# Attention values in a decoder step: both halves of one head's values side by side in one stationary operand

## The chip, the cores and the metric

The kernel runs on one core of one Trainium2 chip. The metric is the device time of one execution in microseconds (us). TensorE is called PE below, VectorE DVE, ScalarE ACT, GpSimd POOL and SyncE SP, as in the profile.

## What is computed

One inference step of a two-layer decoder trunk: 1024 prompt tokens and 64 sample tokens (8 sequences of 8), model width 1024. Layer 0 mixes with sparse attention (8 query heads, 2 key/value heads of width 64, the 256 best keys of each query) beside a pooling mixer, layer 1 with a gated spatial unit, and each layer has a SwiGLU part with 2816 hidden columns. The change touches one product of layer 0, the probabilities times the values of the prompt:

```python
logits = jnp.where(valid, einsum('bnhgd,bnshd->bnhgs', qg, k_sel) * HEAD_DIM ** -0.5, -inf)
p = jax.nn.softmax(logits, axis=-1)
o = jnp.einsum('bnhgs,bnshd->bnhgd', p, v_sel)
```

## The kernel before

The work is cut into two groups of tokens, g = 0 (prompt tokens 0 to 511) and g = 1 (tokens 512 to 1023 and the 64 sample tokens). For each group the kernel runs the attention, then the output projection, then the SwiGLU part of layer 0, layer 1 and its SwiGLU part. Every engine has its own program, and semaphores order them. There is no scheduler: the order of each engine is the order of the code.

All large products are made in three parts. An fp32 number is split into a high part (a copy rounded to the type fp32r, which PE multiplies in one pass) and a low part (the number minus its high part), and PE adds high by high, high by low and low by high into one PSUM bank.

The prompt's attention (`attend`, one per engine) goes through tiles `t` of 128 queries, 0 to 3 in group 0 and 4 to 7 in group 1. A pair of a tile and a key/value head, (t, z) with z = 0 or 1, is called a *section* here: it holds four query heads, and t + 1 blocks `kk` of 128 keys. The table `items(g)` sets the order of the work on all engines:

- `qk`: the logits of one query head, on PE (L899 the mask, L902 the products), then on DVE the row maximum (L1916) and its negative (L1918), on ACT the exponential with its row sum (L1279), on DVE the reciprocal of the sum (L1898, held back for up to three items), on POOL the division of the row (L1618, the tiles `probs_short`, `probs_long_a` and `probs_long_b`). The four heads of the *next* section are put among the first blocks of the present one. They are called heads A, B, C, D below.
- `tr`: one block of the four heads' probabilities is transposed on PE (L912) into one of two PSUM banks, copied by ACT to the high part (L1303, tile `probs_t`), and DVE subtracts to make the low part (L1925, the same tile). The section's first transpose waits until POOL has divided head D.
- `pv`: PE multiplies the block by the values (L919, tile `values_split`) into bank 6 + z. It waits for the low part of its own block; the transpose of the block after it is issued ahead of it.
- `o`: the finished section's result, 64 rows of the bank, is written to `act_split`, the operand of the output projection: the high part by a copy of ACT (L1311), the low part by a subtraction of DVE (L1930). It stands in the *next* section, just behind that section's first `pv`; the last section's stands at the end.

In `pv` the stationary operand is a 128 by 128 block of the values, keys by (both key/value heads, 64 columns each). So PE makes 128 rows for each section, of which `o` takes the 64 of head z. The values are split once per group by ACT (L1264) and POOL (L1592). After the last `o`, group 0 goes on with the output projection (L653), group 1 with the sample tokens' attention (L935 and on), and both wait for it. A matmul of PE is called a product.

## Time and profile before

| | |
|---|---|
| time, median of 3 runs | 2970.72 us (2960.51 to 2972.42) |
| profiled execution: time | 2972.42 us |
| profiled execution: span | 2972.3 us |
| PE busy, products | 2648.4 us (89%) |
| PE busy, weight loads (beside the products) | 2328.3 us |
| DVE, ACT, POOL busy | 1453.8, 995.1, 1250.6 us |
| the 216 products of `pv` (L919), busy | 68.2 us |
| group 0's attention | about 420 to 498 us |
| group 1's attention (prompt part) | about 1592 to 1707 us |

The first column of the profile's group rows is the line of the kernel. "Busy" of a group is the time in which at least one of its instructions ran; a mean is of one instruction. The shares over the whole span say little on this change, since it touches 193 of 2972 us.

### The profile page before, as it was taken

How to read it: one execution, taken by the hardware profiler on the slowest of the kernel's cores; microseconds unless marked ns; L12 is line 12 of the kernel's file. 1: busy time of each engine (PE TensorE's matmuls, PEld its weight loads, DVE VectorE, ACT ScalarE, POOL GpSimd, SP SyncE). 2: the span in 40 equal slices, each digit the busy share in tenths (PEclk: the TensorE clock that was granted, in tenths of full speed). 3: DMA queues.
4: the chain of work that ended last, by engine and by line, in shares of the span. 5: the costliest groups of instructions: out<-in, count | busy, mean ns of one | idle time of the engine just before them, and what ended most of it. 6: DMA issues, size and time to landing. Idle time of an engine off the chain costs nothing.

```text
span 2972.3 us, 43500 instructions
## 1 busy us (share of the span) xinstructions
PE 2648.4 (89%) x15061; PEld 2328.3 (78%) x15065; DVE 1453.8 (49%) x1895; ACT 995.1 (33%) x1450; POOL 1250.6 (42%) x632
## 2 busy tenths in 40 slices
PE   6979767799997887999986897999997987999997
PEld 5669545588886665888865677999997987999997
DVE  3459755898688655312355635221235445220234
ACT  3242444432233344322224534222223334222222
POOL 4434223354553334554544413443443333443441
PEclk9979879799998888999988987999998988999998
DMA  4443211133232211333322121232232211232231
GB/s 120 100 122 83 81 45 32 56 93 105 86 103 81 64 50 57 93 103 94 100 63 85 35 81 50 80 92 76 78 89 60 71 51 45 78 88 78 81 94 51
DMA packets 451740, 230.00 MB, mean 77 GB/s; under 512 B 90588, under 2 KB 443568, under 8 KB 451127
## 3 DMA queue, kind: packets, MB, share of 16 engines
q1 hardware_dynamic: 451647, 228.80, 26.7%
q8 instruction: 53, 0.87, 0.1%
q14 instruction: 40, 0.33, 0.0%
HBM read 213.43 MB, written 15.43 MB: 77 GB/s over the span
## 4 chain that ended last, share of the span: by engine, by line
PE 72%; DVE 16%; issue 5%; ACT 3%; POOL 2%; DMA 1%; SPq 0%; DVEq 0%; ACTq 0%; POOLq 0%
PE psum L653 63%; DVE top L1715 2%; DVE scores L1722 2%; DVE temps L2027 1%; DVE square_sums L1678 1%; DVE resid L2032 1%; PE psum L741 1%; PE psum L685 1%; DVE scores L1860 1%; POOL act_split L1552 1%; DVE probs_t L1925 1%; PE psum L734 1%; PE psum L912 1%; DVE diag_rstd L1687 1%; DVE row_stats L1916 1%
## 5 line engine op out<-in xcount | busy, mean ns | idle before, releaser
L653 PE MATMUL psum<-act_split,w_hi 128*128 128x288 f32 (+1 forms) x6144 | 1368.5, 332 | 28.2 <-POOL act_split L1552 9.5
L1520 POOL TENSOR_TENSOR w_lo<-w_raw,w_hi 128x1024 fp32r<-128x1024 f32 (+1 forms) x336 | 859.5, 2558 | 1234.2 <-ACT w_hi L1096 1234.2
L653 PEld LDWEIGHTS psum<-act_split,w_hi 128*128 128x128 f32 x6144 | 998.0, 191 | 125.5 <-issue 19.1
L1096 ACT ACTIVATE w_hi<-w_raw 128x1024 fp32r<-128x1024 f32 (+1 forms) x336 | 376.9, 1122 | 1419.7 <-PE psum L653 1379.6
L653 PE MATMUL psum<-act_split,w_lo 128*128 128x288 f32 (+1 forms) x3072 | 844.1, 329 | 0.0
L653 PEld LDWEIGHTS psum<-act_split,w_lo 128*128 128x128 f32 x3072 | 527.5, 190 | 41.3
L653 PE MATMUL psum<-hidden_split,w_hi 128*128 128x288 f32 (+1 forms) x2112 | 461.3, 327 | 0.0
L653 PEld LDWEIGHTS psum<-hidden_split,w_hi 128*128 128x128 f32 x2112 | 339.6, 188 | 27.4
L653 PE MATMUL psum<-hidden_split,w_lo 128*128 128x288 f32 (+1 forms) x1056 | 287.7, 327 | 0.0
L1671 DVE TENSOR_TENSOR square_sums<-square_sums,squares 128x512 f32<-128x512 f32 (+1 forms) x80 | 167.9, 2099 | 168.5 <-ACT squares L1360 121.9
L1980 DVE TENSOR_TENSOR temps<-psum,root_of_input 128x512 f32<-128x512 f32 (+1 forms) x88 | 63.5, 721 | 360.0 <-PE psum L653 346.3
L1986 DVE TENSOR_TENSOR temps<-psum,temps 128x512 f32<-128x512 f32 (+1 forms) x88 | 63.4, 720 | 352.1 <-PE psum L653 333.4
L1988 DVE TENSOR_TENSOR hidden_split<-temps,hidden_split 128x512 f32 (+1 forms) x88 | 171.3, 1946 | 92.9 <-ACT hidden_split L1375 92.9
L653 PEld LDWEIGHTS psum<-hidden_split,w_lo 128*128 128x128 f32 x1056 | 179.5, 188 | 13.7
L1722 DVE MATCH_REPLACE8 scores<-top,scores 128x640 f32<-128x640 f32 (+2 forms) x208 | 178.0, 864 | 0.0
L685 PE MATMUL psum<-act_split,w_hi 128*128 128x288 f32 (+1 forms) x384 | 123.0, 417 | 57.5 <-POOL act_split L1552 31.9
L1715 DVE MAX8 top<-scores 128x8 f32<-128x640 f32 (+2 forms) x208 | 170.4, 869 | 2.1
L685 PEld LDWEIGHTS psum<-act_split,w_hi 128*128 128x128 f32 x384 | 78.6, 240 | 82.5 <-POOL act_split L1552 46.5
L1539 POOL TENSOR_TENSOR temps<-temps,root_of_input 128x512 f32<-128x512 f32 (+1 forms) x88 | 119.9, 1363 | 31.3 <-ACT temps L1372 31.2
L1552 POOL TENSOR_TENSOR act_split<-mixed,act_split 128x512 fp32r<-128x512 f32 (+1 forms) x48 | 71.5, 1491 | 110.8 <-ACT mixed L1402 110.8
L1925 DVE TENSOR_TENSOR probs_t<-psum,probs_t 128x512 fp32r<-128x512 f32 x72 | 49.3, 688 | 63.3 <-ACT probs_t L1303 63.0
L919 PE MATMUL psum<-probs_t,values_split 128*128 128x512 f32 x216 | 68.2, 427 | 10.9 <-DVE probs_t L1925 10.8
(240 smaller groups left out, 2392.4 us busy)
## 6 DMA issues: line engine op xcount, KB each, us to landing
w_raw<-in_w_ffn_gate_up SPq DMA_DIRECT2D x352, 256.0 KB, 3.1
w_raw<-in_w_ffn_down SPq DMA_DIRECT2D x64, 384.0 KB, 3.5
w_raw<-in_w_ffn_down SPq DMA_DIRECT2D x64, 320.0 KB, 4.0
w_raw<-in_w_in_even SPq DMA_DIRECT2D x64, 256.0 KB, 3.7
w_raw<-in_w_in_odd SPq DMA_DIRECT2D x64, 256.0 KB, 3.0
w_raw<-in_w_out_odd SPq DMA_DIRECT2D x32, 256.0 KB, 3.1
x_rows<-in_x_prompt SPq DMA_DIRECT2D x8, 512.0 KB, 6.3
w_raw<-in_w_out_even SPq DMA_DIRECT2D x32, 128.0 KB, 2.9
```

What stands on the lines that cost most here:

```text
L653: mm = pe.matmul(PS[:, 2 * p + b, 0:hi - lo], w[:, p, at], x(k)[:, lo:hi], start=(k == 0 and w is WH and x is x_hi), stop=(k == ph.kt - 1 ...
L685: mm = pe.matmul(PS[:, 2 * p + b, 0:hi - lo], w[:, p, at], x(k)[:, lo:hi], start=(k == 0 and w is WH and x is a_hi), stop=(k == ph.kt - 1 ...
L919: mm = pe.matmul(PS[:, 6 + z, :], VS[:, v, kk, :], PT[:, kc % 2, q, :], start=kk == 0 and v == 0 and q == 0, stop=kk == t and v == 1)
L1096: act.activation(WH[:, p, 0:n], WR[:, p, 0:n], ACT.Copy).then_inc(S("w_hi"), 1)
L1520: pool.tensor_tensor(WL[:, p, 0:n], WR[:, p, 0:n], WH[:, p, 0:n].bitcast(F32), ALU.subtract).then_inc(S("w_lo"), 1)
L1539: pool.tensor_tensor(TT[:, 0, 0:T[g]], TT[:, 0, 0:T[g]], RB[:, 0:T[g]], ALU.mult).then_inc(S("gated"), 1)
L1552: pool.tensor_tensor(AR[:, 1, n, 0:T[g]], src, AR[:, 0, n, 0:T[g]].bitcast(F32), ALU.subtract).then_inc(S("a_lo"), 1)
L1671: dve.tensor_tensor(SS[:, 0:T[g]], SS[:, 0:T[g]], SQ[:, p, 0:T[g]], ALU.add).then_inc(S("ss_p"), 1)
L1715: ins_ = dve.max(M8[0:s.shape[0], m, :], s)
L1722: ins_ = dve.match_replace(out=s, in_to_replace=M8[0:s.shape[0], m, :], in_values=s, imm_value=CHOSEN)
L1925: dve.tensor_tensor(PT[:, kc % 2, 1, :], PS[:, 4 + kc % 2, :], PT[:, kc % 2, 0, :].bitcast(F32), ALU.subtract).then_inc(S("pt_lo"), 1)
L1988: dve.tensor_tensor(flat(HR[:, 1, ds(i, 1), 0:T[g]]), TT[:, 1, 0:T[g]], flat(HR[:, 0, ds(i, 1), 0:T[g]].bitcast(F32)), ALU.subtract).then_ ...
```

## The change

The tile `VS` (`values_split`) gets another layout: keys by (block, key/value head, high or low, 64). The stationary operand of `pv` is now the high part and the low part of *one* head's values, side by side. Its 128 columns give, in rows 0 to 63 of the bank, the high values times the probabilities, and in rows 64 to 127 the low values times the probabilities. The moving operand goes through it twice, the high and then the low part of the probabilities: two products per block in place of three. The product of low by low comes with them, which was not computed before.

The two halves of the bank must then be added. In `o`, ACT copies rows 64 to 127 to a new tile `out_low`, DVE adds rows 0 to 63 to it and writes a new tile `out_total`, and from that ACT makes the high part and DVE the low part as before. The new tiles lie over `squares` and `temps`, which are free there.

```diff
-        VS = over("values_split", [P, 2, 8, P], F32R, h_at, 4096)
+        VS = over("values_split", [P, 8, 2, 2, HD], F32R, h_at, 4096)
+        OL = over("out_low", [HD, 2, 512], F32, sq_at, 0)
+        OT = over("out_total", [P, 512], F32, tt_at, 0)
...
@@ PE, pv
-                        for v, q in ((0, 0), (0, 1), (1, 0)):
-                            mm = pe.matmul(PS[:, 6 + z, :], VS[:, v, kk, :], PT[:, kc % 2, q, :],
-                                           start=kk == 0 and v == 0 and q == 0, stop=kk == t and v == 1)
+                        for q in (0, 1):
+                            mm = pe.matmul(PS[:, 6 + z, :], VS[:, kk, z, :, :], PT[:, kc % 2, q, :],
+                                           start=kk == 0 and q == 0, stop=kk == t and q == 1)
...
@@ ACT, o
+                        wait(act, S("o_lo"), 2 * t + z - 1)
+                        act.activation(OL[:, z, :], PS[HD:P, 6 + z, :], ACT.Copy).then_inc(S("o_part"), 1)
+                        act.wait_ge(S("o_sum"), 2 * t + z + 1)
                         act.activation(AR[64 * z:64 * z + 64, 0, 0:4, at],
-                                       PS[64 * z:64 * z + 64, 6 + z, :].rearrange("p (j q) -> p j q", j=4), ACT.Copy).then_inc(S("o_hi"), 1)
+                                       OT[64 * z:64 * z + 64, :].rearrange("p (j q) -> p j q", j=4), ACT.Copy).then_inc(S("o_hi"), 1)
...
@@ DVE, o
-                        dve.wait_ge(S("o_hi"), 2 * t + z + 1)
+                        dve.wait_ge(S("o_part"), 2 * t + z + 1)
+                        dve.tensor_tensor(OT[r, :], PS[0:HD, 6 + z, :], OL[:, z, :], ALU.add).then_inc(S("o_sum"), 1)
+                        dve.wait_ge(S("o_hi"), 2 * t + z + 1)
-                        dve.tensor_tensor(AR[r, 1, 0:4, at], PS[r, 6 + z, :].rearrange("p (j q) -> p j q", j=4),
+                        dve.tensor_tensor(AR[r, 1, 0:4, at], OT[r, :].rearrange("p (j q) -> p j q", j=4),
                                           AR[r, 0, 0:4, at].bitcast(F32), ALU.subtract).then_inc(S("o_lo"), 1)
```

The split of the values by ACT and POOL changes only in its output's layout.

How the instructions of ACT stand in section (5, 0), from its second block on, before (`act_split<-psum` is `o`, `probs_t` the copy of a block, `probs_long_b` the exponential of a head):

```order
581 L1303 ACTIVATE probs_t<-psum 128x512
582 L1279 ACTIVATE probs_long_b,row_stats<-psum,row_stats 128x768
583 L1311 ACTIVATE act_split<-psum 64x4x128
584 L1303 ACTIVATE probs_t<-psum 128x512
585 L1279 ACTIVATE probs_long_b,row_stats<-psum,row_stats 128x768
```

and now:

```order
590 L1306 ACTIVATE probs_t<-psum 128x512
591 L1282 ACTIVATE probs_long_b,row_stats<-psum,row_stats 128x768
592 L1315 ACTIVATE out_low<-psum 64x512
593 L1317 ACTIVATE act_split<-out_total 64x4x128
594 L1306 ACTIVATE probs_t<-psum 128x512
595 L1282 ACTIVATE probs_long_b,row_stats<-psum,row_stats 128x768
```

`o` is two instructions in place of one, with a wait for DVE between them, and the copy of the next block and the exponential of head B stand behind both.

The same place on DVE, before (`row_stats` by TENSOR_REDUCE is a row maximum, by RECIPROCAL the inverse of a row sum):

```order
712 L1916 TENSOR_REDUCE row_stats<-psum 128x1
713 L1918 TENSOR_SCALAR row_stats<-row_stats 128x1
714 L1898 RECIPROCAL row_stats<-row_stats 128x1
715 L1930 TENSOR_TENSOR act_split<-psum,act_split 64x4x128
716 L1925 TENSOR_TENSOR probs_t<-psum,probs_t 128x512
717 L1898 RECIPROCAL row_stats<-row_stats 128x1
718 L1916 TENSOR_REDUCE row_stats<-psum 128x1
```

and now:

```order
721 L1922 TENSOR_REDUCE row_stats<-psum 128x1
722 L1924 TENSOR_SCALAR row_stats<-row_stats 128x1
723 L1904 RECIPROCAL row_stats<-row_stats 128x1
724 L1936 TENSOR_TENSOR out_total<-psum,out_low 64x512
725 L1938 TENSOR_TENSOR act_split<-out_total,act_split 64x4x128
726 L1931 TENSOR_TENSOR probs_t<-psum,probs_t 128x512
727 L1904 RECIPROCAL row_stats<-row_stats 128x1
728 L1922 TENSOR_REDUCE row_stats<-psum 128x1
```

The addition has come in ahead of the subtraction, the subtraction now waits for ACT's second instruction, and head B's reciprocal and head C's maximum stand behind both.

## Rows read from the trace of the kernel before

**Rows 1.** Windows: both attentions, then three stretches of group 0's; busy us (count), clock.
```profile
core 0: us, PE busy (x) PEld busy (x) DVE busy (x) ACT busy (x) POOL busy (x), PEclk, DMA share, GB/s
420.00:498.00 78.00, 51.33 (x228) 37.99 (x230) 41.62 (x123) 37.63 (x94) 30.64 (x38) 0.80 0.09 25
1592.00:1707.00 115.00, 100.83 (x530) 77.86 (x532) 74.97 (x147) 66.19 (x122) 53.62 (x35) 0.98 0.10 28
430.00:440.00 10.00, 6.63 (x25) 5.20 (x25) 3.76 (x14) 3.98 (x12) 3.71 (x5) 0.50 0.11 29
440.00:450.00 10.00, 7.76 (x27) 5.98 (x27) 5.27 (x16) 4.66 (x13) 3.72 (x5) 0.50 0.00 0
450.00:460.00 10.00, 6.07 (x34) 4.71 (x34) 5.37 (x16) 5.61 (x14) 4.58 (x5) 0.96 0.46 132
```

**Rows 2.** Waits of PE within group 1's attention: us in total, times, longest.
```profile
PE psum L919 <- DVE probs_t L1925: 7.8, 19, 1.1
PE psum L912 <- POOL probs_long_a L1618: 7.3, 3, 5.2
PE psum L912 <- POOL probs_long_b L1618: 2.0, 3, 1.1
```

**Rows 3.** Timeline of PE: one block's three products; the last two of them alone.
```profile
1654.56 0.85 PE L919 MATMUL psum<-probs_t,values_split 128*128 128x512 f32 x3
1654.79 0.62 PE L919 MATMUL psum<-probs_t,values_split 128*128 128x512 f32 x2
```

**Rows 4.** Chain of waits through section (5, 0): start us, us, what; then its end.
```profile
1623.21 0.88 DVE row_stats L1916
...
1624.37 0.69 DVE act_split L1930
...
1625.09 0.69 DVE probs_t L1925
...
1625.86 0.87 DVE row_stats L1916
...
1631.00 1.48 POOL probs_long_b L1618
```

**Rows 5.** Timeline around `o` in section (5, 0): start us, us, engine, line, operation.
```profile
1623.03 0.59 ACT L1311 ACTIVATE act_split<-psum 64x512 fp32r<-64x512 f32 x1
1623.64 0.60 ACT L1303 ACTIVATE probs_t<-psum 128x512 fp32r<-128x512 f32 x1
...
1624.30 0.90 ACT L1279 ACTIVATE probs_long_b<-psum,row_stats 128x768 f32<-128x768 f32 x1
...
1624.48 1.47 POOL L1618 TENSOR_TENSOR probs_long_b<-probs_long_b,row_stats 128x768 f32<-128x768 f32 x1 [2.35 <-DVE row_stats L1898]
...
1625.70 0.15 DVE L1898 RECIPROCAL row_stats<-row_stats 128x1 f32<-128x1 f32 x1
```

**Rows 6.** Timeline around `o` in section (0, 1) of group 0.
```profile
435.81 0.57 ACT L1311 ACTIVATE act_split<-psum 64x512 fp32r<-64x512 f32 x1
...
436.28 0.46 ACT L1279 ACTIVATE probs_short<-psum,row_stats 128x256 f32<-128x256 f32 x1
436.41 0.68 DVE L1930 TENSOR_TENSOR act_split<-psum,act_split 64x512 fp32r<-64x512 f32 x1 [0.37 <-ACT act_split L1311]
```

**Rows 7.** One line each: durations in ns, minimum, median and maximum.
```profile
L1272 ACT ACTIVATE queries_split<-queries_tile x16: 615/627/631, 415.3 to 1662.3; 64x512 fp32r<-64x512 f32 x16
L1671 DVE TENSOR_TENSOR square_sums<-square_sums,squares x80: 692/2319/3247, 14.0 to 2943.6; 128x512 f32<-128x512 f32 x40, 128x576 f32<-128x576 f32 x40
```

**Rows 8.** Timeline: a POOL instruction and a DVE one with two SBUF inputs beside it.
```profile
506.50 2.40 POOL L1520 TENSOR_TENSOR w_lo<-w_raw,w_hi 128x1024 fp32r<-128x1024 f32 x1 [17.33 <-ACT w_hi L1096]
...
507.24 2.20 DVE L1671 TENSOR_TENSOR square_sums<-square_sums,squares 128x512 f32<-128x512 f32 x1 [8.83 <-ACT squares L1360]
```

**Rows 9.** Timeline after the last block of group 1: `o`, then the next stage.
```profile
1705.72 0.59 ACT L1311 ACTIVATE act_split<-psum 64x512 fp32r<-64x512 f32 x1 [1.78 <-PE psum L919]
1706.35 0.69 DVE L1930 TENSOR_TENSOR act_split<-psum,act_split 64x512 fp32r<-64x512 f32 x1 [1.68 <-ACT act_split L1311]
1707.14 1.06 PE L935 MATMUL psum<-constants,key_pages 128*128 128x128 f32 x8 [1.46 <-issue]
```

More of the change, by code:

```diff
@@ L1263, in split_keys @@
                         act.activation(KS[64 * r:64 * r + 64, kv, 0, 0:n], KT[64 * kv:64 * kv + 64, 0:n], ACT.Copy).then_inc(S("ks_hi"), 1)
-                act.activation(VS[:, 0, 0:4 * (g + 1), :], VN[:, 0:4 * (g + 1), :], ACT.Copy).then_inc(S("ks_hi"), 1)
+                act.activation(VS[:, 0:4 * (g + 1), :, 0, :], VN[:, 0:4 * (g + 1), :].rearrange("p k (z d) -> p k z d", z=2),
+                               ACT.Copy).then_inc(S("ks_hi"), 1)
             def attend(g):
@@ L1591, in split_keys @@
                 pool.wait_ge(S("ks_hi"), 5 * g + 5)
-                pool.tensor_tensor(VS[:, 1, 0:4 * (g + 1), :], VN[:, 0:4 * (g + 1), :], VS[:, 0, 0:4 * (g + 1), :].bitcast(F32),
-                                   ALU.subtract).then_inc(S("ks_lo"), 1)
+                pool.tensor_tensor(VS[:, 0:4 * (g + 1), :, 1, :], VN[:, 0:4 * (g + 1), :].rearrange("p k (z d) -> p k z d", z=2),
+                                   VS[:, 0:4 * (g + 1), :, 0, :].bitcast(F32), ALU.subtract).then_inc(S("ks_lo"), 1)
                 pool.wait_ge(S("ks_lo"), 5 * g + 5)
```

## The prediction

> **What bounds the kernel now.** I read the windows first. Group 0's attention takes 78 us and PE computes in 51.3 of them; group 1's takes 115 us and PE computes in 100.8 [rows 1]. So fewer products look like a gain in group 1, and DVE (75 of 115) and ACT (66) look free. Then the waits: in group 1 PE waits 7.8 us in `pv` for the low part from DVE, and 9.3 us at the start of sections (7.3 and 2.0) for POOL's division [rows 2]. PE is thus often kept, not keeping. The chain of waits says by whom. Through section (5, 0) it runs on DVE without a gap: maximum of head B at 1623.21, `o` at 1624.37, low part of the block at 1625.09, maximum of head C at 1625.86, in the end POOL's division of head D at 1631.00 to 1632.48, which the next section's first transpose waits for [rows 4]. No product of `pv` is on it. A section lasts as long as this: logits of four heads, maxima, exponentials, reciprocals, four divisions. DVE and ACT are idle at the start and the end of a section and have no slack in its middle, which is where `o` stands.
>
> **The change part by part.** The sum is made against the profiled execution's 2972.42 us, 1.7 us over the median of 2970.72.
>
> *Products removed.* The second and third product of a block take 0.62 us of 0.85, so the second starts 0.23 us after the first: one product is 0.23 us of PE [rows 3]. 72 blocks lose one each: 20 x 0.23 = 4.6 us in group 0, 52 x 0.23 = 12.0 us in group 1, 16.6 together (somewhat more where the clock is at 0.50). That is the most that can be gained. On the path it counts only where PE goes from block to block with no head's logits between: the last section of each group, which prepares no other. There the blocks go in pairs, one `pv` of each pair on the path: 4 blocks give 2 x 0.23 = 0.5 us, 8 blocks 4 x 0.23 = 0.9 us. For section (4, 0), which has no `o`, I add 0.2. Gain: 1.6 us.
>
> *`o` in the middle of a section.* This is 6 sections in group 0 ((0, 1) to (3, 0)) and 6 in group 1 ((4, 1) to (7, 0)). I place the new instructions on the rows of (5, 0) [rows 4, 5]. ACT's copy to `out_low` costs what `o` costs ACT now, 1623.03 to 1623.62. DVE's addition, with one input in PSUM as now, stands where L1930 stands, 1624.37, and takes 0.69, to 1625.06. Until then ACT, which used to copy the next block at 1623.64, stands still. Then come ACT's copy from SBUF, 0.63 by the same form in L1272 [rows 7], to 1625.72; the block's copy, 0.60, to 1626.34; head B's exponential, 0.90 in place of 1624.30, and its sum, to about 1627.3. DVE can take head B's reciprocal at 1627.35 where it did at 1625.70 [rows 5], and head C's maximum right behind. That is 1.65 us later, and everything after it is serial: maximum C, maximum D, exponential, division, next section. By the same working the others of group 1 come to between 1.6 and 2.1, I take 1.7: 6 x 1.7 = 10.2 us.
> In group 0, section (0, 1): the first copy is done at 436.38; DVE adds from 436.41 to 437.09; ACT's second copy ends at 437.75; head D's exponential starts there and not at 436.28, 1.5 us later [rows 6]. The DVE side alone gives 1.3 (0.69 and 0.63 with the semaphores). I take 1.4: 6 x 1.4 = 8.4 us.
> Bounds for one of these twelve: below, 0 (all of it in idle time, as the shares of DVE and ACT in rows 1 would allow); above, 2.1 plus a wait for POOL, next.
>
> *The subtraction's inputs.* L1930 had one input in PSUM; its successor has both in SBUF. The nearest rows are L1671, also with two SBUF inputs: 0.69 us at least, but 2.32 in the median and 3.25 at most [rows 7]. The one at 507.24 ended at 509.44, 0.54 us after the POOL instruction beside it [rows 8]. In group 1, POOL divides head A's row just then (1624.48 to 1625.95 in rows 5), so the subtraction would end at about 1626.5 and the block's low part at 1627.2, just inside the 1627.35 above. I take 0.4 us over all sections; the upper bound is a division of 1.47 us more in each of six, 9 us.
> The Trainium skill (SBUF — State Buffer, Who interferes with whom) says that a DVE instruction with two SBUF inputs and a GpSimd instruction that reads SBUF exclude each other for the whole of an instruction, whichever came first. It thus speaks against this change; without it the sum would be 0.4 us less, by its worst case 9 more.
>
> *`o` in the two last sections.* In (3, 1) and (7, 1) the first copy need not wait long, and the following block comes about 0.4 us later: 0.8 together. After the last block `o` is bare: now 0.59 and 0.69, then PE goes on at 1707.14 [rows 9]. With a copy of 0.59, the addition 0.69, a copy 0.63 and the subtraction 0.69, it is longer by 1.3 us and one hand-over more, say 1.35. Twice: 2.7 us.
>
> *The split of the values* has the same sizes and comes long before the first product that reads it; I cost it at nothing. If the new layout doubled it, the load of queries that PE waits for would still cover it. The new waits for `o_lo` in ACT and PE ask for an `o` two sections back.
>
> Sum: 10.2 + 8.4 + 0.4 + 0.8 + 2.7 - 1.6 = 20.9 us. Against the profiled execution that is 2993.3, against the median 2991.6, so **2992 us**.
>
> **The rivals.**
> *PE bounds (faster than forecast, not slower than before).* If PE's 100.8 of 115 us is what sets group 1, all the removed products come off, 16.6 us, and only the bare ends cost, 2.7: -13.9, 2957 us. For it: PE's share, and that in sections (5, 1), (6, 1) and (7, 0) the chain runs over PE for a stretch. Against it: DVE starts each maximum there the moment the one before is through. It decides if ACT's and DVE's 1.3 us fit before the next logits are ready. Chance 0.07.
> *Half absorbed.* The delay in each of the twelve is only the bare work, about 0.6 us, and the later blocks give back 3 us in all: 7.2 + 3.5 - 1.6 - 3 = 6, 2977 us. For it: the section's last blocks have slack on DVE. Against it: their slack lies behind the delayed maxima. Chance 0.15.
> *The clock.* Group 0 runs at 0.50 (1.2 GHz) from 430 to 450 and is at 0.96 (2.4 GHz is 1.00) from 450 on, right after the slice in which PE was busiest, 7.76 of 10 us [rows 1]. With fewer products and longer waits the rise may come only with the output projection. A product is 0.287 us at half clock (7.76 / 27) and 0.179 after (6.07 / 34); of the 228 products some 150 lie behind 450 us: 16 us of PE, about half on the path, so +8: 3000 us. In group 1 PE would still be busy in 89 of about 125 us, more than the 6.07 of 10 that held the clock, so I leave that out. Chance 0.13.
> The Trainium skill (TensorE: Matmul & The Clock Gate, HAM oscillation — how this bites in real kernels) tells of kernels whose clock falls again in each gap between bursts of products. By that rule group 0 would not have risen at 450 us amid its gaps, so the trace does not bear it out fully here.
> *The port.* The subtraction waits for POOL each time, or holds it up: +9, 3001 us. Chance 0.07.
> That the change does not do what it says I exclude: the order shows two products per block and the longer `o` in both programs.
>
> **How the numbers follow.** The forecast has 0.58, with 15 to 26 us around its 21 (each of the twelve between 1.2 and 2.1). A measurement of this kernel tells about 0.5% from no change, 14.9 us, so slower starts at 2985.6. Of the forecast I leave 0.07 under that. Slower: 0.51 + 0.13 + 0.07 = 0.71. Faster by over 0.5% is under 2955.9: 0.03 of the 0.07 of the first rival. Within: 0.26. The range, 2974 to 3004, takes in the clock, the port and most of the half absorbed case with the scatter of the runs (2960.5 to 2972.4), and leaves out the first rival.
>
> **What would show it.** Sections of group 0 1.2 to 1.5 us longer, those of group 1 1.6 to 2.1 us, both attentions together about 213 us in place of 193; L919's successor at 144 products; PE's wait for POOL at the starts of sections grown, to over 15 us in group 1; the chain through a section going over ACT's second copy or the addition; nothing changed outside. I am wrong if the section's length does not grow, if the subtraction takes over 1.5 us on average, or if the granted clock after 450 us stays at half.

## The result and the profile after

The changed kernel takes 3005.93 us in the median of 4 runs (2996.08 to 3009.39), beside 2971.57 us for the kernel before (4 runs, 2960.51 to 2976.09). The ratio is 1.0121, interval 1.0087 to 1.0156: slower, as forecast, by 34.4 us where 20.9 were forecast, and 1.9 us above the upper end of the range.

The two profiled executions are compared by their spans, 2972.3 and 3003.9 us, which is 31.6 us more. The busy times after the change:

```profile
PE 2653.1 (88%) x14990; PEld 2329.1 (78%) x14993; DVE 1467.3 (49%) x1911; ACT 1005.9 (33%) x1466; POOL 1250.5 (42%) x632
```

PE has 72 products fewer, and its busy time is not shorter (2653.1 us, before 2648.4). So a part of what is left must run more slowly. The line of `pv` by itself (durations in ns: minimum, median, maximum), and PE's waits in group 1's attention, which answer to [rows 2] (there 7.8, 7.3 and 2.0 us):

```profile
L921 PE MATMUL psum<-probs_t,values_split x144: 387/397/796, 428.5 to 1733.7; 128*128 128x512 f32 x144
```

```profile
PE psum L921 <- DVE probs_t L1931: 12.8, 19, 1.6
PE psum L914 <- POOL probs_long_a L1624: 9.0, 4, 5.5
PE psum L914 <- POOL probs_long_b L1624: 3.1, 3, 1.5
```

144 products in place of 216. PE's wait for the low part has grown from 7.8 to 12.8 us, and that for POOL from 9.3 to 12.1.

The next view is cut at the moments at which POOL ends a section's fourth division, the end of a section as the prediction described it. The first six rows are sections (0, 1) to (3, 0) of group 0, the others (4, 1) to (7, 0) of group 1:

```profile
core 0: us, PE busy (x) PEld busy (x) DVE busy (x) ACT busy (x) POOL busy (x), PEclk, DMA share, GB/s
430.82:440.99 10.17, 4.87 (x18) 3.61 (x18) 4.44 (x15) 4.66 (x12) 3.71 (x6) 0.50 0.10 27
440.99:451.79 10.80, 5.16 (x24) 4.09 (x24) 5.95 (x17) 5.08 (x13) 3.71 (x6) 0.82 0.00 0
451.79:463.03 11.24, 5.85 (x24) 4.54 (x24) 5.62 (x16) 5.74 (x13) 4.58 (x6) 0.80 0.41 119
463.03:475.08 12.05, 7.75 (x30) 6.00 (x30) 7.11 (x18) 6.10 (x14) 4.57 (x5) 0.77 0.00 0
475.08:487.55 12.47, 7.70 (x29) 5.39 (x30) 6.89 (x17) 6.64 (x14) 5.42 (x5) 0.79 0.00 1
487.55:500.44 12.89, 9.57 (x36) 6.48 (x36) 7.65 (x18) 6.50 (x14) 4.16 (x4) 0.76 0.01 1
1620.89:1634.66 13.77, 9.42 (x54) 7.40 (x54) 9.06 (x19) 8.55 (x16) 7.15 (x6) 1.00 0.07 20
1634.66:1649.98 15.32, 10.57 (x60) 8.19 (x60) 10.38 (x21) 9.01 (x17) 7.16 (x6) 0.99 0.01 2
1649.98:1666.74 16.76, 12.67 (x60) 9.58 (x60) 10.45 (x20) 9.39 (x17) 7.99 (x5) 0.91 0.06 16
1666.74:1685.59 18.85, 15.39 (x66) 11.49 (x66) 12.06 (x22) 9.97 (x18) 7.99 (x5) 0.82 0.15 43
1685.59:1702.14 16.55, 13.02 (x66) 9.30 (x66) 11.84 (x21) 10.41 (x18) 8.86 (x6) 1.00 0.09 24
1702.14:1720.75 18.61, 14.27 (x71) 10.16 (x72) 12.62 (x22) 10.49 (x18) 7.57 (x4) 1.00 0.02 6
```

Two things are to be seen. Each of these twelve sections is longer than before, and the clock (last column but two) is well below 1.00 in eight of them, all of group 0 and (5, 1) and (6, 0). The same cuts in the kernel before, and in experiment e3 below, in which the clock was higher over both attentions, but not in (1, 0) and hardly in (2, 0):

| section | before: us, clock | change: longer by, clock | e3: longer by, clock | forecast |
|---|---|---|---|---|
| (0, 1) | 8.64, 0.50 | 1.53, 0.50 | 1.37, 0.99 | 1.4 |
| (1, 0) | 9.81, 0.50 | 0.99, 0.82 | 1.06, 0.53 | 1.4 |
| (1, 1) | 9.83, 0.88 | 1.41, 0.80 | 0.52, 0.98 | 1.4 |
| (2, 0) | 10.35, 1.00 | 1.70, 0.77 | 1.71, 0.78 | 1.4 |
| (2, 1) | 10.20, 1.00 | 2.27, 0.79 | 2.20, 0.95 | 1.4 |
| (3, 0) | 10.36, 1.00 | 2.53, 0.76 | 1.28, 1.00 | 1.4 |
| (4, 1) | 12.20, 1.00 | 1.57, 1.00 | 1.58, 1.00 | 1.7 |
| (5, 0) | 13.62, 1.00 | 1.70, 0.99 | 1.68, 1.00 | 1.7 |
| (5, 1) | 14.03, 1.00 | 2.73, 0.91 | 1.55, 1.00 | 1.7 |
| (6, 0) | 14.44, 1.00 | 4.41, 0.82 | 1.81, 1.00 | 1.7 |
| (6, 1) | 15.03, 1.00 | 1.52, 1.00 | 2.42, 1.00 | 1.7 |
| (7, 0) | 16.98, 1.00 | 1.63, 1.00 | 2.23, 1.00 | 1.7 |

**The hand-over.** The timeline around `o` in section (5, 0), which answers to [rows 5]:

```profile
1638.83 0.59 ACT L1315 ACTIVATE out_low<-psum 64x512 f32<-64x512 f32 x1
...
1640.18 0.69 DVE L1936 TENSOR_TENSOR out_total<-psum,out_low 64x512 f32<-64x512 f32 x1
...
1640.30 1.47 POOL L1624 TENSOR_TENSOR probs_long_b<-probs_long_b,row_stats 128x768 f32<-128x768 f32 x1 [2.35 <-DVE row_stats L1904]
...
1640.90 0.63 ACT L1317 ACTIVATE act_split<-out_total 64x512 fp32r<-64x512 f32 x1 [1.48 <-DVE out_total L1936]
1641.55 0.60 ACT L1306 ACTIVATE probs_t<-psum 128x512 fp32r<-128x512 f32 x1
1641.56 0.75 DVE L1938 TENSOR_TENSOR act_split<-out_total,act_split 64x512 fp32r<-64x512 f32 x1 [0.69 <-ACT act_split L1317]
1642.17 0.90 ACT L1282 ACTIVATE probs_long_b<-psum,row_stats 128x768 f32<-128x768 f32 x1
...
1643.28 0.94 DVE L1922 TENSOR_REDUCE row_stats<-psum 128x1 f32<-128x768 f32 x1
```

ACT writes `out_low` from 1638.83 to 1639.42 and then stands for 1.48 us, until DVE, which first takes head B's maximum, has added. Head B's exponential, for which the negative maximum is there from 1640.07 on, starts at 1642.17, and head C's maximum at 1643.28. From ACT's first instruction of `o` to head C's maximum it is 4.45 us; before, it was 1623.03 to 1625.86 [rows 4, 5], 2.83. That is 1.62 us, with 1.65 forecast by the same steps. The chain of waits of the change goes over just these instructions:

```profile
1641.55 0.60 ACT probs_t L1306
...
1642.17 1.00 ACT probs_long_b L1282 x2
...
1643.36 0.87 DVE row_stats L1922
```

**The clock.** Where it falls in group 1 the timeline of PE shows, at the end of section (5, 0), and the windows around it:

```profile
1646.77 0.73 PE L921 MATMUL psum<-probs_t,values_split 128*128 128x512 f32 x2 [0.53 <-DVE probs_t L1931]
1648.35 0.73 PE L921 MATMUL psum<-probs_t,values_split 128*128 128x512 f32 x2 [0.84 <-DVE probs_t L1931]
1650.03 1.11 PE L914 MATMUL psum<-constants,probs_long_b 128*128 128x128 f32 x4 [0.95 <-POOL probs_long_b L1624]
...
1651.38 1.90 PE L904 MATMUL psum<-keys_split,queries_split 128*128 128x448 f32 x4
```

```profile
1640.00:1650.00 10.00, 5.44 (x29) 3.65 (x27) 6.49 (x15) 5.72 (x11) 5.87 (x4) 0.98 0.00 0
1650.00:1653.00 3.00, 2.97 (x10) 2.52 (x11) 0.69 (x1) 1.22 (x2) 0.43 (x1) 0.50 0.00 0
1653.00:1660.00 7.00, 5.63 (x33) 4.43 (x32) 5.91 (x11) 4.99 (x9) 2.84 (x3) 1.00 0.13 37
```

After three waits in a row of 0.53, 0.84 and 0.95 us, with two products between one and the next, PE runs at 0.50, 1.2 GHz, for some 3 us: the four products of 1651.38 take 1.90 us. Afterwards it is at 1.00, 2.4 GHz, again. In the kernel before no section of this group after (4, 0) is below 1.00. The row of waits alone does not decide it: in e2 below, PE's same three waits at the end of (5, 0) are 0.54, 0.84 and 0.96 us, and the clock stays at 1.00. And the fall within (6, 0), from 1676.9 to 1680.3 us, came after one wait of 2.20 us in the section's middle.

**After the last block.** The timeline that answers to [rows 9]:

```profile
1734.11 0.59 ACT L1315 ACTIVATE out_low<-psum 64x512 f32<-64x512 f32 x1 [1.54 <-PE psum L921]
1734.73 0.68 DVE L1936 TENSOR_TENSOR out_total<-psum,out_low 64x512 f32<-64x512 f32 x1 [1.45 <-ACT out_low L1315]
...
1735.45 0.63 ACT L1317 ACTIVATE act_split<-out_total 64x512 fp32r<-64x512 f32 x1 [0.75 <-DVE out_total L1936]
...
1736.11 0.69 DVE L1938 TENSOR_TENSOR act_split<-out_total,act_split 64x512 fp32r<-64x512 f32 x1 [0.69 <-ACT act_split L1317]
...
1736.90 1.94 PE L937 MATMUL psum<-constants,key_pages 128*128 128x128 f32 x8 [2.83 <-issue]
```

From `o` to PE's next product it is 2.79 us, before 1.42: 1.37 us more, 1.35 forecast. But the eight products that follow now take 1.94 us, before 1.06: after the gap of 2.83 us in PE (before 1.46) it stands at half clock.

### The profile page after: what moved, and what is told of

Its sections match the earlier page's. It is cut to its first block, busy times and chain, and to the rows that moved or that the text cites. A ratio compares the mean times of both kernels' runs of the same rounds, so it can differ in the third digit from the quotient of the medians.

```text
span 3003.9 us, 43402 instructions
## 1 busy us (share of the span) xinstructions
PE 2653.1 (88%) x14990; PEld 2329.1 (78%) x14993; DVE 1467.3 (49%) x1911; ACT 1005.9 (33%) x1466; POOL 1250.5 (42%) x632
## 4 chain that ended last, share of the span: by engine, by line
PE 73%; DVE 15%; issue 4%; ACT 4%; POOL 2%; DMA 1%; SPq 0%; DVEq 0%; ACTq 0%; POOLq 0%
PE psum L655 63%; DVE temps L2035 1%; DVE top L1721 1%; DVE square_sums L1684 1%; DVE resid L2040 1%; DVE scores L1728 1%; PE psum L743 1%; PE psum L687 1%; DVE scores L1866 1%; PE psum L914 1%; DVE row_stats L1922 1%; POOL act_split L1558 1%; PE psum L736 1%; PE psum L904 1%; DVE diag_rstd L1693 1%
## 5 line engine op out<-in xcount | busy, mean ns | idle before, releaser
L2040 DVE SCALAR_TENSOR_TENSOR resid<-temps,gains,resid 128x512 f32<-128x512 f32 (+1 forms) x64 | 75.5, 1179 | 1.0
```

The source lines that it names most:

```text
L2040: dve.scalar_tensor_tensor(out=X[:, n, 0:T[g]], in0=TT[:, n % 2, 0:T[g]], scalar=gain(base, layer, n), in1=X[:, n, 0:T[g]], op0=ALU.mult, ...
```

## The experiments

Each was timed in five rounds beside the kernel before. The ratios stand with their 95% intervals; the kernel before had a median of 2974.06 us beside e1 to e4, 2974.28 beside e5 to e8 and 2975.60 beside e9 to e12.

### e1 and e2: one half of the change each

e1 is the kernel before with the new `o` of ACT and DVE and its two tiles, and three products as before:

```diff
@@ ACT, o (DVE as in the change)
+                        wait(act, S("o_lo"), 2 * t + z - 1)
+                        act.activation(OL[:, z, :], PS[HD:P, 6 + z, :], ACT.Copy).then_inc(S("o_part"), 1)
+                        act.wait_ge(S("o_sum"), 2 * t + z + 1)
                         act.activation(AR[64 * z:64 * z + 64, 0, 0:4, at],
-                                       PS[64 * z:64 * z + 64, 6 + z, :].rearrange("p (j q) -> p j q", j=4), ACT.Copy).then_inc(S("o_hi"), 1)
+                                       OT[64 * z:64 * z + 64, :].rearrange("p (j q) -> p j q", j=4), ACT.Copy).then_inc(S("o_hi"), 1)
```

> The kernel before with its three products per block, and only `o` lengthened as in the change: ACT copies rows 64 to 127 of the bank, DVE adds rows 0 to 63, and both splits follow. (The rows added are those of the two heads, so this computes another output.) Hand-over theory: the longer `o` is the whole loss, about 1.7 us in each of 12 sections and 1.35 us at each of the two ends, +22 us against before. Clock theory: the longer `o` costs the same 22 us, but of the change's 34 us some 10 come from TensorE's clock, which falls in the longer gaps; PE has 16.6 us more of products here, so the clock holds better: +20 to +26 us, below the change, with a granted clock above the change's 0.74 to 0.83 in 450 to 500 us. If the removed products were worth anything on the path, this kernel would be slower than the change, over +34.

Measured: 2997.76 us, ratio 1.0093 (1.0057 to 1.0130), runs from 2983.0 to 3018.2. Its six sections of group 1 at clock 0.89 to 1.00 take 98.95 us in all, before 86.30, the change 99.86. The clock falls here too, with all three products in: (4, 1) and (5, 0) ran at 0.89 and 0.90, 15.11 and 16.91 us long.

e2 is the change with the old `o`:

```diff
@@ ACT, o (DVE's subtraction is the old one too)
-                        wait(act, S("o_lo"), 2 * t + z - 1)
-                        act.activation(OL[:, z, :], PS[HD:P, 6 + z, :], ACT.Copy).then_inc(S("o_part"), 1)
-                        act.wait_ge(S("o_sum"), 2 * t + z + 1)
                         act.activation(AR[64 * z:64 * z + 64, 0, 0:4, at],
-                                       OT[64 * z:64 * z + 64, :].rearrange("p (j q) -> p j q", j=4), ACT.Copy).then_inc(S("o_hi"), 1)
+                                       PS[64 * z:64 * z + 64, 6 + z, :].rearrange("p (j q) -> p j q", j=4), ACT.Copy).then_inc(S("o_hi"), 1)
```

> The change's layout and its two products per block, with the old short `o` (copy and subtraction from rows 64z to 64z + 63, the halves are not added, so another output is computed). Hand-over theory: the products lie off the path but for the last sections, -2 us against before. Clock theory: sparser products alone already let the clock fall in group 0, -2 to +6 us, with the granted clock of 450 to 500 us below before's 0.96 to 1.00. Theory that PE bounds group 1: -12 to -17 us.

Measured: 2976.50 us, ratio 1.0025 (1.0008 to 1.0042), runs from 2961.3 to 2992.1. Two of its sections, (6, 0) and (7, 0):

```profile
1650.13:1664.56 14.43, 12.59 (x66) 9.30 (x66) 10.73 (x21) 9.46 (x17) 8.01 (x5) 1.00 0.15 42
...
1679.35:1696.33 16.98, 14.06 (x72) 10.07 (x72) 11.50 (x21) 9.87 (x17) 7.58 (x4) 1.00 0.02 7
```

Before they took 14.44 and 16.98 us, with PE busy in 13.51 and 15.77 of them. So 0.9 and 1.7 us of PE's work are gone, and the sections are not shorter. Only in the two last sections is something gained: from the last full section's end to the next stage's first product it is 13.03 us in place of 14.19 in group 1, and 7.86 in place of 8.56 in group 0. That is 1.9 us, with 1.4 forecast for these two places.

It follows that the longer `o` alone makes most of the loss (+24 us in the median, 17 to 39 by its interval, of the change's 34), and that the removed products are worth about 2 us where the clock stays. In the median they are worth nothing, 2.4 us longer: e2's twelve runs spread over 31 us, and the five above 2980 us all have a mean clock of 0.922 or less. All twelve lie at 0.918 to 0.927, the 23 runs of the kernel before beside them at 0.925 to 0.930. So with fewer products the mean clock is lower in part of the executions. e2's profiled execution is its fastest, 2961.34 us; most of what it gains over the profiled kernel before lies in a later stage (see the last section), not in the attention.

### e3 and e8: PE kept busy where it waits for POOL

Here six products whose result nobody reads stand ahead of the first transpose of 14 sections, so that PE works while POOL still divides:

```diff
+                        wait(pe, S("pt_lo"), kc - 1)
                         if kk == 0:
+                            for _ in range(6 if kc > kbase(4 * g, 0) else 0):
+                                pe.matmul(PS[:, 4 + kc % 2, :], VS[:, 0, 0, :, :], KS[:, 0, 0, 0:512], start=True, stop=True)
                             pe.wait_ge(S("p_norm"), 8 * t + 4 * z + 4)
-                        wait(pe, S("pt_lo"), kc - 1)
```

> The change, and ahead of a section's first transpose (14 of 16 sections), while PE would wait for POOL's division of head D, six idle products of 128 by 512 into the bank that the transposes then overwrite: 1.3 us at full clock, 2.6 at half, in gaps of 2 to 3 us. Hand-over theory alone: no gain, 0 to +5 us against the change. Clock theory: the granted clock in both attentions goes to 0.95 or more and the change's excess of about 10 us goes, +22 to +26 against before.

Measured: 3000.70 us, 26.6 over the kernel before in the median, ratio 1.0103 (1.0081 to 1.0125). By the ratios e3 can't be told from the change (1.0121 and, in e12, 1.0106); what it shows is in its sections. The six runs fall apart by their clock: three at 0.931 with 2992.6, 2996.3 and 2998.5 us, three at 0.922 to 0.924 with 3003.0 to 3012.7. The profiled one is of the first kind. At the place where the change's clock fell, PE's timeline in it reads:

```profile
1643.60 0.72 PE L923 MATMUL psum<-probs_t,values_split 128*128 128x512 f32 x2 [0.84 <-DVE probs_t L1933]
1644.16 1.52 PE L913 MATMUL psum<-keys_split,values_split 128*128 128x512 f32 x6
1645.52 0.60 PE L916 MATMUL psum<-constants,probs_long_b 128*128 128x128 f32 x4
...
1646.17 1.14 PE L904 MATMUL psum<-keys_split,queries_split 128*128 128x448 f32 x4
```

The six products fill the wait, the transposes take 0.60 us in place of 1.11 and the four products 1.14 in place of 1.90; sections (5, 1) and (6, 0) come to 15.58 and 16.25 us at full clock. This is the column of e3 in the table above: (5, 1), (6, 0) and (3, 0) are back at 1.3 to 1.8 us over before. In (6, 1) and (7, 0), where the clock held anyway, the idle products cost 0.9 and 0.6 us, so the others may hold some of that cost too. The clock did not reach the expected 0.95 everywhere: (1, 0) ran at 0.53 and (2, 0) at 0.78. The span of this execution is 22.2 us over before, near the forecast's 20.9.

e8 has more of them (group 0 six, and two ahead of every other transpose; group 1 four):

> The change with more idle products than e3 where e3's clock still fell: in group 0 six ahead of a section's first transpose and two ahead of every other, in group 1 four in place of six (in e3 the two last sections of group 1 were 0.9 and 0.6 us longer than in the change at the same clock of 1.00, which the six products cost). Clock theory: all sections but the first at 0.95 to 1.00, the excess over the forecast gone: +18 to +23 us against before. Hand-over theory alone: as the change, +34, or worse by the added products.

Measured: 3005.03 us, ratio 1.0093 (1.0058 to 1.0128). It did not hold the clock. Its two attentions together are no longer than e3's (group 1's seven sections 110.2 us, e3's 111.2), but the stage after them began at 0.50:

```profile
1740.00:1760.00 20.00, 20.00 (x72) 12.23 (x71) 4.69 (x13) 5.14 (x15) 0.00 (x0) 0.50 0.62 179
```

The kernel before has 0.83 in the first 20 us after the attention. So e3 shows what sections cost at full clock in group 1, and e8 that filling the gaps of one stage does not secure the clock of the next. Neither is a cure.

### e4, e5 and e9: `o` in another place

In e4, the change's `o` is moved from behind the section's first `pv` to the section's end, behind the exponential and the reciprocal of head D, and cut into two items. For group 0 and 1 the order of all engines changes in this way:

```diff
-                        if kk == 0 and done:
-                            out.append(done)
-                    done = ("o", t, kv, 0)
-            return out + [done]
+                        if kk == 0 and done and not ahead:
+                            out += done
+                    if done and ahead:
+                        out += done
+                    done = [(x, t, kv, 0) for x in ("oa", "ob")]
+            return out + done
```

`oa` is ACT's copy to `out_low` and DVE's addition, `ob` the rest. e5 is the same move in the kernel before, with its one item.

> The change with `o` moved: not behind the first block of the next section but behind its last block's copy and split, head D's exponential and reciprocal ahead of it (the two last sections keep the old place). ACT and DVE have about 2.5 us there until the next section's first block, and `o` takes 2.6. Hand-over theory: nothing of `o` is left on the path in 12 sections; since the old `o` too had about 0.7 us of DVE there (8 us in all), this comes to +2 - 8 = -6 us against before, bounds -10 and +6. Theory that `o` costs wherever it stands: +20 to +34. Clock theory adds up to 10 us to the first.

> The kernel before (three products, short `o`) with `o` moved to the end of the next section as in e4. Hand-over theory: `o` held DVE 0.67 us in the middle of 12 sections; out of there, -5 to -8 us against before, if the clock stays (before had 0.928 over the span). Theory that the place of `o` does not matter: 0. Against e4, which has 16.6 us less of products and a longer `o` in the same place: if the removed products are worth nothing and only feed the clock's fall, this one is faster than e4's +4, with a mean clock above e4's 0.922.

Measured: e4 2976.37 us, ratio 1.0014 (0.9997 to 1.0031); e5 2974.21 us, ratio 1.0014 (0.9989 to 1.0039). In both, ACT's held-back exponential and DVE's held-back reciprocals are issued ahead of it. The move takes some 29 us off the change and nothing off the kernel before. Two of e4's sections, (6, 1) and (7, 0):

```profile
1667.58:1682.23 14.65, 12.92 (x66) 9.34 (x66) 11.67 (x21) 11.14 (x19) 8.85 (x6) 1.00 0.16 45
1682.23:1698.44 16.21, 13.98 (x72) 10.12 (x72) 12.21 (x22) 10.65 (x19) 7.57 (x4) 1.00 0.03 7
```

They are shorter than before (15.03 and 16.98), with the longer `o` in them, since it now runs while POOL divides. But the other five of group 1 run at 0.83 to 0.91, and its seven sections take 102.7 us, before 100.4. What the order gives, the clock takes back; in e5, too, the seven take 102.8 us, three of them at 0.83 to 0.88.

In e9 `oa` stays where `o` was and `ob` comes one block later, so that ACT copies the next block while DVE adds:

```diff
+                        if kk == 0 and done:
+                            out.append(done[0])
+                        if kk == min(1, t) and done:
+                            out.append(done[1])
```

> The change with `o` cut in two items: ACT's copy to `out_low` and DVE's addition stay behind the next section's first block, ACT's high part and DVE's low part come one block later (two sections of one block keep both together). The work is the same and stays in the middle of the section; only the standing still of ACT (0.75 us and more) and of DVE (0.69 us) goes. If the waits are the loss: the sections lose 0.7 to 1.0 us of their excess of 1.55 to 1.8, that is -8 to -12 us against the change, and more by the clock. If the added work is: -2 to +2.

Measured: 2999.49 us, ratio 1.0078 (1.0048 to 1.0107), at mean clocks of 0.915 to 0.922. Section (6, 0) ran at full clock:

```profile
1662.91:1678.24 15.33, 12.65 (x66) 9.31 (x66) 11.50 (x22) 10.10 (x18) 8.43 (x5) 1.00 0.15 44
```

That is 0.89 us over before, where the change's `o` cost 1.81 (e3). (4, 1), (6, 1) and (7, 0), at 0.94 to 0.97, are 0.16, 0.33 and 0.43 us over before, where the change has 1.57, 1.52 and 1.63 at full clock. So half of the price, and in three of these four sections over 70%, goes when the two engines need not stand still for each other; the bare work is at most half. The gain of this on the whole kernel, 6.5 us beside e12 where 8 to 12 were expected, is within the scatter of the runs: (5, 0) and (5, 1) ran at 0.81 and 0.89.

### e6, e7, e10, e11: late `o` and idle products together

e6 is e4 with five idle products at the start of each of group 0's sections but the first, and three in group 1; e11 is e4 with the five of group 0 alone; e7 is e5 with the five of group 0; e10 is the kernel before with these five and nothing else:

```diff
+                        wait(pe, S("pt_lo"), kc - 1)
+                        idle = 0 if kc == kbase(4 * g, 0) else (5, 0)[g] if kk == 0 else 0 * (g == 0)
+                        for _ in range(idle):
+                            pe.matmul(PS[:, 4 + kc % 2, :], VS[:, 0, 0, :], KS[:, 0, 0, 0:512], start=True, stop=True)
                         if kk == 0:
                             pe.wait_ge(S("p_norm"), 8 * t + 4 * z + 4)
-                        wait(pe, S("pt_lo"), kc - 1)
```

> The change with the late `o` of e4, and idle products ahead of a section's first transpose: five in group 0 (gaps of 1.9 us on average in e4), three in group 1 (gaps about 1 us). Clock theory: e4's sections were as short as before's or shorter where the clock was at 1.00 and longer where it was at 0.84 to 0.91; with the clock held, -5 to -12 us against before, mean clock 0.928 or more. Without it: the same as e4, +4, or up to 5 worse for the products.

> e5 with five idle products ahead of the first transpose in group 0 only. Clock theory: before ran the sections (0, 1) to (1, 1) at 0.50 too; a section at half clock is 0.5 to 1.2 us longer, so -2 to -4 us against e5. Otherwise 0 to +3.

> The kernel before with nothing but the five idle products ahead of a section's first transpose in group 0, as in e7 (which also has the late `o` and came out at -0.36%). Clock theory: sections (0, 1) to (1, 1) get full clock, -3 to -6 us against before. If e7's gain was the late `o`'s: 0.

> The change with the late `o` and the idle products in group 0 alone: e7 but for two products per block and the longer `o`. If the removed products are worth nothing on the path, e7's time plus 1.35 us at each end, that is -8 to -11 us against before; if fewer products let the clock fall in group 1, as in e4 (0.87 to 0.91 there), 0 to +4; if they are worth something, below e7, under -15.

| | us | ratio (95%) | mean clock of its runs |
|---|---|---|---|
| e6: change, late `o`, idle products in both groups | 2976.66 | 1.0010 (0.9992 to 1.0027) | 0.925 to 0.932 |
| e11: change, late `o`, idle products in group 0 | 2983.87 | 1.0025 (1.0002 to 1.0047) | 0.922 to 0.926 |
| e7: before, late `o`, idle products in group 0 | 2961.19 | 0.9964 (0.9947 to 0.9982) | 0.931 to 0.935 |
| e10: before, idle products in group 0 | 2965.01 | 0.9968 (0.9951 to 0.9986) | 0.932 to 0.936 |

The windows of e10 in group 0's attention answer to [rows 1] (0.50, 0.50 and 0.96 there):

```profile
430.00:440.00 10.00, 6.45 (x42) 5.11 (x40) 3.86 (x15) 4.63 (x13) 3.71 (x5) 0.99 0.10 27
440.00:450.00 10.00, 6.99 (x33) 5.72 (x32) 5.47 (x17) 4.63 (x13) 3.71 (x5) 0.83 0.01 2
450.00:460.00 10.00, 6.38 (x34) 4.60 (x32) 5.79 (x19) 5.56 (x14) 5.26 (x6) 1.00 0.46 132
```

The kernel before starts its attention at half clock; with the idle products it does not, group 0's sections (0, 1) to (3, 0) take 58.3 us in place of 59.2, and the runs lie closer together (2961.8 to 2970.1). So e10 and e7 beat both kernels, by a third of a per cent. Whether the late `o` adds anything to e7 the two ratios can't tell. e11 differs from e7 by the change's part alone, two products and the longer `o`, and is 22.7 us slower in the median (the runs of the kernel before beside the two differ by 1.3), although its `o` is out of the way: group 1 ran two sections, (5, 0) and (6, 0), at 0.89 and 0.81 (14.14 and 16.20 us; e7 13.34 and 14.15), and the stage after it, 1698 to 1738 us, at 0.63. Its runs have mean clocks of 0.922 to 0.926, e7's 0.931 to 0.935. Which of the two parts lowers the clock here, the lighter load of PE or the longer ends, no run separates.

Several expectations were missed here. e5 was to gain 5 to 8 us and gained nothing. e6 was to gain 5 to 12 us: in its profiled execution the attentions' sections are 5.2 us shorter than before's, yet its median is 2.4 us over before. e7 and e10 gained more than was expected of the clock in group 0 (13.1 and 10.6 us in the median), and e11 lost 8.3 where 4 was the most.

### e12: the change once more

> The change itself once more, beside e9 to e11 on the same chip: +34 us against before by both theories; by the clock theory its runs lie on a line with the mean granted clock, 2 us for 0.001, and none reaches before's 0.928.

Measured: 3006.00 us, ratio 1.0106 (1.0074 to 1.0139), six runs from 3002.6 to 3008.6. Its sections are those of the first profile: group 0's six 69.7 us (69.6), group 1's seven 112.5 (112.8), with (5, 1) and (6, 0) again below full clock, both at 0.91. The fall of the clock there is no accident of one execution.

## Why the prediction was right, and where it was short

*What bounds the kernel: right.* No product of `pv` is on the chain through a section. e2 shows it: 66 and 72 PE instructions in place of 73 and 80, and the same 14.43 and 16.98 us.

*The delay of a section in group 1, 1.7 us: right.* At full clock the six are 1.57, 1.70, 1.55, 1.81, 1.52 and 1.63 us longer (the third and fourth from e3, the others from the change): 9.8 us, forecast 10.2. The path through (5, 0) was the one foreseen.

*The delay in group 0, 1.4 us: near in sum, and partly by luck.* (0, 1) is 1.53 us longer at 0.50 in both kernels, (3, 0) 1.28 at 1.00 in e3. e3's six together are 8.1 us longer, forecast 8.4, but they lie between 0.52 and 2.20 and their clocks are not before's, so errors cancel in the sum. In the change itself it was 10.4.

*The subtraction with two inputs in SBUF: right.* All sixteen in one row:

```profile
L1938 DVE TENSOR_TENSOR act_split<-out_total,act_split x16: 683/689/1291, 438.8 to 1736.1; 64x512 fp32r<-64x512 f32 x16
```

The median is 0.69 us as before, the longest 1.29. The longer ones are the six in the sections of group 1: each began while POOL divided, and each ended 0.54 to 0.55 us after the division's end, as the row at 507.24 did in [rows 8]. The longest, in (6, 1):

```profile
1691.24 1.89 POOL L1624 TENSOR_TENSOR probs_long_a<-probs_long_a,row_stats 128x1024 f32<-128x1024 f32 x1 [2.23 <-DVE row_stats L1904]
...
1692.38 1.29 DVE L1938 TENSOR_TENSOR act_split<-out_total,act_split 64x512 fp32r<-64x512 f32 x1 [0.70 <-ACT act_split L1317]
```

None of the other ten met a division, and none took over 0.69. So the rival of the port had the mechanism right, a wait in each section of group 1, but not the size: 0.06 to 0.61 us each, 1.9 in all, nowhere the 1.47 of a whole division. It hardly reached the path: (6, 1), with the longest wait, grew by 1.52 us, and (5, 0), with 0.06, by 1.70. The Trainium skill (SBUF — State Buffer, Who interferes with whom) has the later of two such instructions blocked for the whole of the other. The trace agrees that the later one is held up. With a block for the whole division it would end 0.69 us after the division's end, and it ended after 0.54; POOL's spans are rough, so the difference of 0.15 says little.

*The last sections and the bare `o`: right, with the clock left aside.* Forecast 0.8 + 2.7 less 0.5 and 0.9 for the products, 2.1 us; e3 is 1.23 and 1.26 us longer in the two stretches, 2.5. The change's are 2.56 and 1.96 longer, 4.5, the rest being half clock.

*The products removed, −1.6: right in size.* e2's two ends gave 1.9 in place of 1.4. What the term left out is that with fewer products the clock was lower in part of e2's runs; that belongs to the next point.

*The clock, set to 0 in the sum: the step that failed.* The terms as e3's profiled execution has them, at a mean clock of 0.931 (before 0.928), add up to 9.8 + 8.1 + 2.5 − 0.4 (section (4, 0), by e3) = 20.0 us, with 20.9 forecast. The profiled span grew by 31.6, so 11.6 are left, and by the medians 34.4 − 20.0 = 14.4. They lie in group 0's sections (10.4 − 8.1 = 2.3), in (5, 1) and (6, 0) (13.6 − 9.8 = 3.8), in the two ends (4.5 − 2.5 = 2.0) and in the stages after them (1.5 and 1.8); a further 0.9 stands before the attention's first section and is not the change's, and (4, 0) gave 0.7 back. The prediction had this as a rival, for group 0 alone, with +8 us and 0.13, and said of group 1 "so I leave that out", since PE would be busy in 89 of 125 us. Both the placing and the chance were wrong. It was not one thing or the other: the clock's loss came on top of the forecast's delays, which make PE's gaps longer. The mean busy share did not tell either: PE is busy in 85.8 us of the 112.8 of group 1's sections in the change, and the clock fell three times among them after (4, 0), each time after waits. That the clock accounts for the 11.6 us is read from where they lie, in the stretches with a lower clock; e3, the run made to test it, took back (5, 1) and (6, 0), but its time can't be told from the change's.

*The rule on the clock.* In group 0 the granted clock is 0.76 to 0.80 in every section from (1, 1) on, where before it was 0.88 to 1.00. The prediction had weighed against this the Trainium skill (TensorE: Matmul & The Clock Gate, HAM oscillation — how this bites in real kernels), by which the clock falls again in gaps between bursts of products. After the change the trace agrees with it: PE waits 3.90 us for POOL just ahead of (2, 0), before 2.30, and the section takes 12.05 us at 0.77, before 10.35 at 1.00. Other falls here came after shorter waits, such as the 2.20 us in (6, 0).

*What was said would show it.* Sections, count of products, the chain over ACT's second copy: as said. The two attentions were to grow by 20 us together; from POOL's fourth division to the next stage's first product they take 87.7 and 128.9 us, before 74.8 and 114.6, 27.3 more. PE's wait for POOL in group 1 was to pass 15 us and came to 12.1; the waits went to the low part instead, 12.8. "Nothing changed outside" was wrong by the stages right after the attentions, which began at a lower clock.

Open is why the clock falls in one execution and not in another of the same kernel, why it held in e2 after the same three waits, and how the last few microseconds of the loss divide among stages outside the attention.

## What to carry to other kernels

Where two engines hand one small result to and fro in the middle of an in-order stream, count what stands still behind each hand-over, not the instructions: here an addition and a copy, 1.3 us, cost 1.5 to 1.8 us per section in the middle, and at the section's end, beside POOL's division, nothing that could be measured. Fewer products on an engine that waits were worth nothing by themselves here, and they made its gaps longer. Where PE works in bursts with waits between them, put a term for its clock into the sum with a range, read from the waits that the change makes longer and from the start of the next stage, and not from the mean share of busy time.

## What the runs showed that was not expected

The scatter from run to run goes in part with the mean clock. The kernel before, the same instructions each time, took 2996.9 and 2998.4 us at mean clocks of 0.921 and 0.919, and 2968 to 2973 beside them at 0.930 to 0.932. But at 0.927 to 0.930 its runs lie anywhere from 2960.8 to 2980.0.

One part of the rest is in the traces. In a long stretch of group 1 in which PE never rests, the same 128x288 products stand 133 ns apart in the kernel before and 130 in e7, both at the full granted clock:

```profile
1957.00:2057.00 100.00, 100.00 (x752) 100.00 (x751) 9.10 (x7) 23.72 (x27) 39.63 (x15) 1.00 0.29 84
...
1950.00:2050.00 100.00, 100.00 (x771) 100.00 (x770) 11.15 (x8) 23.83 (x27) 41.63 (x16) 1.00 0.29 84
```

The first row is of before, the second of e7. One such stretch of some 360 us ran at the quicker pace in the profiled executions of e2, e6 and e7, and in none of the other eleven. From the sample tokens' attention to the end e2 and e7 take 1250 us, before and e10 1265, at mean clocks of 0.945 to 0.947; by the counts of the two rows the quick stretch makes about 9 of these 15 us. The cause is open. The edits do not touch these stretches, and e6 and e7 have the quick one in one place, e2 in another.

Products that compute nothing made the tuned kernel faster: 5 at the start of each of 7 sections, in e10, and 10.6 us less (0.9968, 0.9951 to 0.9986). Only 0.9 us of it lies in group 0's own sections. In the profiled executions, 6.9 us apart, another 6.6 lie between the two attentions (1088.3 us at a mean clock of 0.938, before 1094.8 at 0.927). Its runs also lack the long ones.

A gap of 2.83 us in PE was followed by half clock at the end of both attentions in the change (eight products in 1.94 us), and in e3, after the same 2.83 us and with idle products ahead, once by half clock (group 0) and once not (1.06 us for the eight in group 1). So the length of one gap alone does not tell.
